# A hybrid convolution and linear-attention block: residual, final norm and store in the convolution's fp32 buffer, gate chain begun one tile earlier

## The reference

```python
h = rms_norm(x, norm_g)
proj = h @ w_in    # c_val, c_gate, c_z, q, k, v, g_lr (16 wide), g_r, m_conv, m_gla
u = c_val * sigmoid(c_gate)
u = depthwise_causal_conv31(u) + conv_b
y_conv = (silu(layer_norm(u)) * silu(c_z)) @ w_conv_out
log_a = log_sigmoid(g_lr @ gate_w2 + gate_b) / 16      # forget gate, per key channel
o = gla_chunked(q, k, v, log_a)   # decayed linear attention, 4 heads; needs exp(+-cumsum(log_a))
y_gla = (rms_norm(o) * silu(g_r)) @ w_gla_out
y = sigmoid(m_conv) * y_conv + sigmoid(m_gla) * y_gla
out = rms_norm(x + y @ w_out, final_g)
```

## Time and profile before

| | us |
|---|---|
| median of 3 runs (lowest, highest) | 1926.79 (1925.39, 1927.14) |
| the profiled execution | 1925.04 |
| its span, core 5, the slowest | 1923.5 |
| the fastest core's span, core 4 | 1907.1 |
| tile 3 to tile 4, first convolution matmul to first convolution matmul | 208.15 |
| first convolution matmul that goes on after the long wait in tile 0 | 301.79 |
| DMA: median from issue to landing of a weight unit, `usc`, one shift, a store | 4.0, 6.9, 5.5, 6.3 |

### The profile page before, as it was taken

How to read it: one execution, slowest core, us unless ns; L and a number is a source line. 1 busy time by engine, 2 the same in 40 slices (tenths; PEclk the granted TensorE clock), 3 DMA queues, 4 the chain that set the end, 5 groups by cost and what they waited for, 6 DMA issues and landing times.

```text
span 1923.5 us, 29181 instructions; the slowest of 8 cores (1907.1 to 1923.5 us)
## 1 busy us (share of the span) xinstructions
PE 1523.7 (79%) x9440; PEld 723.7 (38%) x9440; DVE 643.8 (33%) x991; ACT 655.3 (34%) x1161; POOL 365.2 (19%) x618
## 2 busy tenths in 40 slices
PE   0354006998899889998899889988999889988996
PEld 0121002543344334543354334433454335433442
DVE  1002002433354333432443335433343244332533
ACT  1102002531454125521553145412552155314531
POOL 1101002221032102220222103210222022210311
PEclk9876557998899999999899989999999989998998
DMA  6999998456845495558745594549455874568452
GB/s 119 143 158 147 113 112 232 147 181 181 228 130 188 132 253 157 159 159 227 196 148 176 175 239 130 191 129 279 131 159 159 233 191 147 179 188 226 126 152 74
DMA packets 173795, 326.76 MB, mean 170 GB/s; under 512 B 19776, under 2 KB 60992, under 8 KB 172864
## 3 DMA queue, kind: packets, MB, share of 16 engines
q1 hardware_dynamic: 172224, 299.33, 54.4%
q0 software_dynamic: 1424, 25.56, 11.8%
HBM read 324.69 MB, written 51.12 MB: 195 GB/s over the span
## 4 chain that ended last, share of the span: by engine, by line
PE 60%; DMA 9%; DVE 9%; SPq 8%; ACT 5%; issue 5%; POOL 2%; another core or an unknown queue 0%; DVEq 0%; POOLq 0%; ACTq 0%
PE ps_pb L324 28%; PE ps_pb L334 12%; PE ps_pb L527 8%; PE ps_pb L415 6%; DMA usc<-sb_u 3%; SPq L294 3%; SPq L406 3%; DMA out<-sb_FP 2%; DVE sb_FP L500 2%; DMA w_b<-w 2%; DMA sb_xa<-x 2%; DVE sb_big L468 2%; ACT sb_FP L684 1%; PE ps_pb L660 1%; DVE sb_big L617 1%
## 5 line engine op out<-in xcount | busy, mean ns | idle before, releaser
L324 PE MATMUL ps_pb<-sb_hT,sb_wn 128*128 128x512 bf16 x3136 | 724.2, 387 | 98.8 <-DVE sb_FP L679 48.7
L324 PEld LDWEIGHTS ps_pb<-sb_hT,sb_wn 128*128 128x128 bf16 x3136 | 308.8, 99 | 476.5 <-issue 139.2
L415 PE MATMUL ps_pb<-sb_big,sb_wn 128*32 128x512 bf16 x2048 | 144.3, 431 | 186.5 <-DMA sb_wn<-w_b 120.8
L334 PE MATMUL ps_pb<-sb_big,sb_wn 128*128 128x512 bf16 x1024 | 237.3, 379 | 9.9 <-DVE sb_big L617 9.9
L527 PE MATMUL ps_pb<-sb_wn,sb_hT 128*128 128x512 bf16 x1024 | 227.9, 382 | 9.2 <-DVE sb_u L394 9.2
L454 POOL TENSOR_TENSOR sb_U<-sb_U,sb_FP 128x512 f32<-128x512 f32 x64 | 90.2, 1438 | 471.8 <-DVE sb_FP L440 471.8
L415 PEld LDWEIGHTS ps_pb<-sb_big,sb_wn 128*32 128x32 bf16 x2048 | 62.9, 106 | 259.4 <-issue 221.4
L527 PEld LDWEIGHTS ps_pb<-sb_wn,sb_hT 128*128 128x128 bf16 x1024 | 100.7, 98 | 132.3 <-issue 13.2
L334 PEld LDWEIGHTS ps_pb<-sb_big,sb_wn 128*128 128x128 bf16 x1024 | 98.1, 98 | 124.1 <-issue 13.6
L794 POOL TENSOR_TENSOR sb_yb<-sb_FP 128x512 bf16<-128x512 f32 x64 | 81.0, 1265 | 208.6 <-DVE sb_FP L791 208.5
L394 DVE SCALAR_TENSOR_TENSOR sb_u<-sb_FP,ps_pb 128x512 bf16<-128x512 f32 x64 | 44.0, 687 | 228.2 <-PE ps_pb L324 134.0
(11 more groups left out here) (86 smaller groups left out, 1420.9 us busy)
## 6 DMA issues: line engine op xcount, KB each, us to landing
sb_wn<-w_b SPq DMA_DIRECT2D x776, 256.0 KB, 4.0
sb_big<-usc SPq DMA_DIRECT2D x256, 135.0 KB, 5.5
w_b<-w POOLq DMA_DIRECT2D x17, 1024.0 KB, 54.1
sb_xa<-x SPq DMA_DIRECT2D x32, 512.0 KB, 4.1
sb_FP<-x SPq DMA_DIRECT2D x32, 512.0 KB, 4.7
out<-sb_FP SPq DMA_DIRECT2D x32, 512.0 KB, 6.3
usc<-sb_u SPq DMA_DIRECT2D x64, 136.0 KB, 6.9
w_b<-w POOLq DMA_DIRECT2D x13, 512.0 KB, 27.3
```

The costliest lines, as they stand in the source:

```text
L324: S.op("pe", lambda e, bi=bi, kc=kc, wap=wap: e.matmul(pb[bi][:], lhsT=wap[:, kc * 128:(kc + 1) * 128], rhs=hT[:, hbuf, kc, :], start=(kc ...
L334: S.op("pe", lambda e, bi=bi, kc=kc, wap=wap: e.matmul(pb[bi][:], lhsT=wap[:, kc * 128:(kc + 1) * 128], rhs=src[:, kc, :], start=(kc == 0) ...
L415: S.op("pe", lambda e, cbk=cbk, j=j, b=b, c=c, wap=wap: e.matmul(pb[cbk][32 * b:32 * b + 32, :], lhsT=wap[:, b * 256 + j * 32:b * 256 + j ...
```

## The change

- Residual, square, scale and store of `wout` work in `U1`, in place: `xr_load` brings x into `U1`, four separate blocks, issued in the attention stage after blocks 2 and 3 (two each). Square writes its unused result to `HP`. All four stores are issued in the next tile's GLU stage: block 0 after GLU block 0, block 1 after 1, blocks 2 and 3 after 2.
- `wout` runs over the output's halves first: all four token blocks for half 0, one addition each, then all four for half 1, each followed by `fin` (Square, POOL, scale).
- The low-rank gate projection no longer is a unit: its weights come with the constants (`wglr`, 32 columns a row block), and 8 matmuls in four column groups between two PE drains do it; `gw2` is repeated for the four groups. There are 96 units.
- `gate_in` of the next tile stands at the start of `wout`, `gate_z` with Exp and now Ln after two blocks of half 0. The scans stand after GLU blocks 0 to 3, the subtraction is split into four after blocks 4 to 7, and `decay_exp` follows. Tile 0's stand ahead of the loop. The two wide Exp are issued ahead of the small one.
- The first half of V is evicted by VectorE alone.

```diff
         def gate_in(t):
-            bi = proj_fm(t, U_GLR, t % 2)
+            hbuf = t % 2
+            bi = next_pbank()
+            S.op("pe", lambda e: e.drain())
+            for kc in range(8):
+                q = kc % 4
+                S.op("pe", lambda e, bi=bi, kc=kc, q=q: e.matmul(
+                    pb[bi][32 * q:32 * q + 32, :], lhsT=wglr[:, kc * 32:kc * 32 + 32], rhs=hT[:, hbuf, kc, :],
+                    start=(kc < 4), stop=(kc >= 4), tile_position=(0, 32 * q)),
+                    reads=[B["wglr"], B["hT"][hbuf]], writes=[PB[bi]])
+            S.op("pe", lambda e: e.drain())
             S.op("act", lambda e, bi=bi: e.activation(out=glr[:], in_=pb[bi][:], func=AF.Copy),
                  reads=[PB[bi]], writes=[B["glr"]])
...
+                S.op("act", lambda e, bi=bi, h=h: e.activation(out=FP[:, 4 + h, :], in_=pb[bi][:], func=AF.Exp,
+                                                               scale=-1.0, bias=pp[:, 32 + h:33 + h]),
+                     reads=[PB[bi], B["pp"]], writes=[B["FP"][4 + h]])
+            f4 = FP[:, 4:8, :].rearrange("p a t -> p (a t)")
+            S.op("act", lambda e: e.activation(out=f4, in_=f4, func=AF.Ln, bias=1.0),
+                 reads=B["FP"][4:8], writes=B["FP"][4:8])
+
+        x4 = FP[:, 0:4, :].rearrange("p a t -> p (a t)")
+        f4 = FP[:, 4:8, :].rearrange("p a t -> p (a t)")
+        f3 = f4.rearrange("p (a t) -> p a t", a=16)
+        x3 = x4.rearrange("p (a t) -> p a t", a=16)
+        X4, F4 = B["FP"][0:4], B["FP"][4:8]
+
+        def decay_scan(h):
+            S.op("dve", lambda e: e.tensor_tensor_scan(
+                out=FP[:, 4 + h, :], data0=scanm[:], data1=FP[:, 4 + h, :], initial=0.0, op0=ALU.mult, op1=ALU.add),
+                reads=[F4[h], B["scanm"]], writes=[F4[h]])
+
+        def decay_sub(h):
+            a = slice(4 * h, 4 * h + 4)
+            S.op("dve", lambda e: e.tensor_tensor(out=x3[:, a, :], in0=f3[:, a, :],
+                                                  in1=f3[:, a, 63:64].to_broadcast([128, 4, 128]),
+                                                  op=ALU.subtract), reads=[F4[h]], writes=[X4[h]])
+
+        def decay_exp():
...
+            S.op("act", lambda e: e.activation(out=f4, in_=x4, func=AF.Exp, scale=1.0 / 16.0), reads=X4, writes=F4)
+            S.op("act", lambda e: e.activation(out=x4, in_=x4, func=AF.Exp, scale=-1.0 / 16.0), reads=X4, writes=X4)
             S.op("act", lambda e: e.activation(out=gar[:], in_=gar[:], func=AF.Exp, scale=-1.0 / 16.0),
                  reads=[B["gar"]], writes=[B["gar"]])
-            S.op("act", lambda e: e.activation(out=f4, in_=x4, func=AF.Exp, scale=-1.0 / 16.0), reads=X4, writes=F4)
-            S.op("act", lambda e: e.activation(out=x4, in_=x4, func=AF.Exp, scale=1.0 / 16.0), reads=X4, writes=X4)
...
-                if split and s % 2 == 0:
+                if split and (half == 0 or s % 2 == 0):
...
+        def u1v(s):
+            return U1[:, 2 * s:2 * s + 2, :].rearrange("p a t -> p (a t)")
+            S.op("sp", lambda e: e.dma_start(out=u1v(s), in_=x_d[r0:r0 + 128, :]),
+                 writes=B["U1"][2 * s:2 * s + 2], dma_sem=xr_sems[s])
+            S.op("sp", lambda e: e.dma_start(out=out_d[r0:r0 + 128, :], in_=u1v(s)),
+                 reads=B["U1"][2 * s:2 * s + 2], writes=[B["outdone"][s]], dma_sem=out_sems[s])
+
+        def fin(t, s):
+            col = 8 + (t * 4 + s) % 8
+            ub = B["U1"][2 * s:2 * s + 2]
+            hv = HP[:, 0:2, :].rearrange("p a t -> p (a t)")
+            S.op("act", lambda e: e.activation(out=hv, in_=u1v(s), func=AF.Square, accum_out=ssx[:, col:col + 1]),
+                 reads=ub, writes=[B["HP"][0], B["HP"][1], B["ssx"][col]])
+            S.op("pool", lambda e: e.tensor_scalar(
+                out=ssx[:, col:col + 1], in0=ssx[:, col:col + 1], scalar1=1.0 / D, scalar2=EPS,
+                op0=ALU.mult, op1=ALU.add), reads=[B["ssx"][col]], writes=[B["ssx"][col]])
+            S.op("pool", lambda e: e.tensor_tensor(
+                out=ssx[:, col:col + 1], in0=ssx[:, col:col + 1], in1=pp[:, 26:27], op=ALU.pow),
+                reads=[B["ssx"][col], B["pp"]], writes=[B["ssx"][col]])
+            S.op("dve", lambda e: e.scalar_tensor_tensor(
+                out=u1v(s), in0=u1v(s), scalar=ssx[:, col:col + 1], in1=Gf[:], op0=ALU.mult, op1=ALU.mult),
+                reads=ub + [B["ssx"][col], B["Gf"]], writes=ub)
...
+        def wout(t, more):
+            def mm(bi, sl, s, kc):
+                wap, wbuf = sl[kc // 2]
                 S.op("pe", lambda e: e.matmul(
                     pb[bi][:], lhsT=yb[:, kc, s * 128:(s + 1) * 128],
                     rhs=wap[:, (kc % 2) * 512:(kc % 2) * 512 + 512], start=(kc == 0), stop=(kc == 7)),
                     reads=[wbuf, B["yb"][kc]], writes=[PB[bi]])
 
+            def add(bi, half, s):
+                ub = B["U1"][2 * s + half]
+                S.op("dve", lambda e: e.scalar_tensor_tensor(
+                    out=U1[:, 2 * s + half, :], in0=pb[bi][:], scalar=0.5, in1=U1[:, 2 * s + half, :],
+                    op0=ALU.mult, op1=ALU.add), reads=[PB[bi], ub], writes=[ub])
+
+            if more:
+                gate_in(t + 1)
+            sl = units(t, U_WO(0), 4)
+            b01 = [next_pbank(), next_pbank()]
+            for s in range(2):
+                for kc in range(7):
+                    mm(b01[s], sl, s, kc)
+            for s in range(2):
+                mm(b01[s], sl, s, 7)
+                add(b01[s], 0, s)
+            if more:
+                gate_z(t + 1)
+            for s in (2, 3):
+                bi = next_pbank()
+                for kc in range(8):
+                    mm(bi, sl, s, kc)
+                add(bi, 0, s)
+            sl = units(t, U_WO(1), 4)
             for s in range(4):
+                bi = next_pbank()
+                for kc in range(8):
+                    mm(bi, sl, s, kc)
+                add(bi, 1, s)
+                fin(t, s)
...
                 glu(t, c)
-                if t > 0 and c == 0:
-                    store(t - 1, 3)
+                if c < 4:
+                    decay_scan(c)
+                else:
+                    decay_sub(c - 4)
+                if t > 0 and c in (0, 1, 2):
+                    store(t - 1, c)
+                    if c == 2:
+                        store(t - 1, 3)
                 if c >= 1:
                     shift(c - 1)
             if t == 0:
                 issue_casts(N_U)
-            gate_in(t)
+            decay_exp()
             shift(7)
             wide_tm(t, U_V(0), vT, B["vT"], AF.Copy, True)
-            gate_z(t)
-            gate_decay(t)
             wide_tm(t, U_V(1), vT, B["vT"], AF.Copy, True)
...
-            xr_load(t, 0)
-            xr_load(t, 1)
+                if s >= 2:
+                    xr_load(t, 2 * s - 4)
+                    xr_load(t, 2 * s - 3)
```

More of the change, by code:

```diff
@@ L224, in mk @@
                 B[name] = [Buf("%s%d" % (name, i)) for i in range(n)]
-        for nm in ["cst", "identb", "maskb", "onesb", "scanm", "Gn", "Gf", "pp", "gw2", "glr",
+        for nm in ["cst", "identb", "maskb", "onesb", "scanm", "Gn", "Gf", "pp", "gw2", "glr", "wglr",
                    "tail", "gar", "junk"]:
@@ L234, in build_nc @@
         mk("w_b", N_U)
-        mk("outdone", 2)
+        mk("outdone", 4)
         B["Rbf"] = [[Buf("Rbf%d_%d" % (i, h)) for h in range(4)] for i in range(2)]
@@ L274, in build_nc @@
         S.op("dve", lambda e: e.tensor_copy(out=maskb[:], in_=cst[:, 128:256]), reads=[B["cst"]], writes=[B["maskb"]])
+        S.op("dve", lambda e: e.tensor_copy(out=wglr[:], in_=cst[:, 256:512]), reads=[B["cst"]], writes=[B["wglr"]])
         S.op("dve", lambda e: e.tensor_scalar(out=pp[:, 32:36], in0=pp[:, 32:36], scalar1=-1.0, scalar2=0.0,
@@ L375, in pre_pe @@
                 reads=[PB[6]], writes=[B["hT"][hbuf]])
-        xr_sems = [newsem("xr0"), newsem("xr1")]
-        out_sems = [newsem("o0"), newsem("o1")]
+        xr_sems = [newsem("xr%d" % i) for i in range(4)]
+        out_sems = [newsem("o%d" % i) for i in range(4)]
         u4_sems = [[newsem("u4s_%d_%d" % (i, g)) for g in range(4)] for i in range(8)]
@@ L487, in gate_z @@
                      reads=[B["glr"], B["gw2"]], writes=[PB[bi]])
-                S.op("act", lambda e, bi=bi, h=h: e.activation(out=FP[:, h, :], in_=pb[bi][:], func=AF.Exp, scale=-1.0,
-                                                               bias=pp[:, 32 + h:33 + h]),
-                     reads=[PB[bi], B["pp"]], writes=[B["FP"][h]])
-        def gate_decay(t):
-            f4 = FP[:, 0:4, :].rearrange("p a t -> p (a t)")
-            x4 = FP[:, 4:8, :].rearrange("p a t -> p (a t)")
-            f3 = f4.rearrange("p (a t) -> p a t", a=16)
-            x3 = x4.rearrange("p (a t) -> p a t", a=16)
-            F4, X4 = B["FP"][0:4], B["FP"][4:8]
-            S.op("act", lambda e: e.activation(out=f4, in_=f4, func=AF.Ln, bias=1.0), reads=F4, writes=F4)
-            for h in range(4):
```

(31 more changed lines are left out.)

72 lines of the change are left out of this document (15 added, 57 removed).

## The result

| | before | after |
|---|---|---|
| median (lowest to highest) | 1926.65 (1925.39 to 1927.14), 4 runs | 1858.39 (1854.75 to 1880.22), 4 runs |
| span of the slowest core, profiled execution | 1923.5, core 5 | 1856.7, core 2 |
| spans of the eight cores | 1907.1 to 1923.5 | 1835.5 to 1856.7 |
| granted clock of the slowest core | 0.915 | 0.936 |

The ratio is 0.967, 95% interval 0.9596 to 0.9745. The changed kernel is 68 us faster, where the prediction had 85: 1858 lies in its range of 1820 to 1880, 17 us above its 1841. Times of the experiments are medians of the runs within 1.5% of the kernel's fastest; in the others four or all eight cores were granted a lower clock and took some per cent longer.

A forecast was written before the change was run, and what follows sets the result against it. PE, busy 79%, was taken as the bound, stopped in two gaps at each of seven crossings. 80.5 us there, 2.8 in tile 0 and 1.8 at the end sum to 85 saved: 1841 forecast, range 1820 to 1880.

The forecast's parts named there:

- The second gap: PE's 7.93 us stop before the convolution; moving the gate chain out of the V stage was to gain 12.5 us a crossing.
- the slow clock at the convolution's start: Half-speed clock after the stop before the convolution; its end was to gain 2.4 us a crossing.
- The 0.5 taken for transfers: Convolution waiting for its shifted copies; 0.5 us lost per crossing, between 0 and 5.
- The first gap: PE's 6.93 us stop in the GLU stage; a store's wait was to become 4.7 and 2.6 us for VectorE's order.
- the in-place chain: Residual, square and scale in place in wout; the store's wait goes, VectorE's order replaces it, 0.5 us worse a crossing.
- 11.5 us a crossing: Net gain from tile to tile: 12.5 - 0.5 - 0.5, times 7 crossings, 80.5 us.
- tile 0: First tile's long wait for casts; one unit fewer gives 2.4 us and shift(7) passing one load 0.4, together 2.8.
- Table loads: Two more ScalarE table loads a tile, four in all, hidden at zero cost; without cover 1.3 us a tile.
- Rival 2: The u4 transfers take over the convolution's wait, 3.5 us plus 2.4 of clock a crossing; 1883, chance 0.18.
- Rival 3: Both PE gaps go, another 7.3 + 1.0 us a crossing; 1783, chance 0.08.
- Rivals 4: Stores in the GLU stage choke the shifts, so the kernel gets slower; 1981, chance 0.05.
- 5: Nothing gained, the convolution would wait for the shifts behind VectorE anyway; 1925, chance 0.03.

The follow-up runs named there:

- e3: Changed kernel with the gate chain back in the V stage and the first half of V evicted by both engines; 1877.28, ratio 0.9785.
- e6: Kernel before the change with only the PSUM bank ring of a tile started four banks later; 1880.79, ratio 0.9776.
- e7: e3 with the bank ring started two banks later, so the first GLU units take the late banks; two runs, 1896.93 and 1893.15.
- e5: The changed kernel again, unedited; 1851.83, ratio 0.9635.
- e8: Changed kernel with 8 unused weight units more cast behind tile 0's last cast; 1867.4, ratio 0.9711.
- e2: Changed kernel with the PSUM bank ring of a tile started two banks later, VectorE's order kept; 1814.88, ratio 0.9457.
- e1: Changed kernel with each block's scale issued after the next block's addition in the second half of the output projection; 1789.4, ratio 0.9328.
- e4: Changed kernel with each store issued right after its scale in the output projection, none in the GLU stage; 1851.9, ratio 0.9673.
- e9: e1 with each store issued right after its scale in the output projection, none in the GLU stage; 1786.26, ratio 0.93.

## Why the prediction held, and where it was off

**The second gap, right.** L415 no longer waits for the value evictions. V to C fell by 8.10; the prediction's terms for it are 0.87 + 7.93 - 0.4 = 8.4. The difference is the pause at PE's drain before the convolution, 0.74 instead of 0.41; what makes this drain the longer one, no run here tells. Of the 2.4 for the slow clock at the convolution's start, C to Q shows 1.68. The 0.5 taken for transfers did not come (0.01). Short waits between C and Q grew by 0.3 us on the mean, and the remaining 0.4 I can't name. That the gain goes with the gate work and its place is shown by e3, where the wait is back at 7.9; e6 shows that another start of the ring only moves it. e3 undoes two things at once, though, the place of the gate work and VectorE's eviction of the first half of V, and no run parts these.

**The first gap, right in mechanism and size.** Predicted: additions 4.3 apart, measured 4.30, 4.57 and 4.29. Waits of 4.7 and 2.6, measured 4.63 and 1.13, because the first unit at half speed fills part of the second. Predicted: the second block's first unit (CG(1)) 26.7 us after W, measured 1064.24 + 1.73 - 1039.54 = 26.4. The clock loss behind the second wait was taken as 1.0; it is 0 in the crossing shown and 1.3 on average (31.53 - 30.2). The clock of 1.00 before the fall that the prediction names stands in none of the earlier trace rows; the trace before has it, 1.00 from 1083 to 1084 and 0.50 from 1085 to 1086 on core 5. Square of block 0 at 1051.03 was not held by Ln, which ended at 1050.11.

```profile
1048.20 1.91 ACT L502 ACTIVATE sb_FP<-sb_FP 128x2048 f32<-128x2048 f32 x1
1051.03 1.06 ACT L671 ACTIVATE sb_HP<-sb_U 128x1024 bf16<-128x1024 f32 x1 [0.92 <-DVE sb_U L693]
```

**Wrong: to whom the gain was credited.** The prediction's step is the in-place chain, "0.5 us worse", with all 12.5 given to the gate work. The 0.5 was worked out with the gate's matmuls and its five allocations in it. e3 shows the parts: the in-place half alone gains 5.3 us a crossing, and moving the gate work adds 4.4 to that. Moving it saves 9.6 us from V to Q (44.09 in e3, 34.54 after) and costs 4.6 from W to V (47.20, 51.80) and 0.5 ahead of W. Of the 4.6, 0.5 are PE's own gate work (1.8 us from W to V here, 1.3 in e3) and 2.1 the longer wait for the additions ((39.3 - 24.3) / 7), because the GLU units get the late banks first. The rest, 2.0, I put down to the slow clock in and behind a longer idle stretch. e7 reproduces those waits from the ring alone. With the banks dealt as the prediction had them, e7's W to V is 50.67 against 52.14 before: the in-place half with the small gate unit (0.4) is 1.5 us better there and 2.4 over the crossing, not 0.5 worse. The sum hardly suffered, since both parts were changed at once. Anyone who took only half of this change by the prediction's account would have been misled.

**Wrong in size: 11.5 us a crossing.** By the means it is 9.7 (207.29 to 197.63), 1.8 less. Of this 0.9 is the choice of the core: on core 5 the stretch from W to V took 53.1 us at this crossing (with a gap of 6.9; it is 6.8 to 7.2 in five of that core's seven, where the others have about 6), on the mean 52.1. The prediction's figure for this stretch, 53.1 - 1.73 + 0.5 = 51.9, was met: 51.8. Another 0.4 is the drain ahead of the gate projection, which stands before W, so that the terms from W on missed it (the branches' stretch grew from 43.42 to 43.83). The rest is 0.3 at the drain before the convolution and 0.2 between C and Q. On the slowest cores it is 72.2 / 7 = 10.3, hence 72 us instead of 80.5 (208.1 on core 5 before and 197.8 on core 2 after, means of their seven).

**Wrong in size: tile 0.** Predicted 2.8 gained. On the mean over the cores `wout` of tile 0 begins at 431.2 instead of 433.3. That is no proof of a gain: the changed kernel again (e5) has 427.6 there, and e6, with all 97 units, 426.3. And the kernel's time is that of the slowest core, and on core 2 tile 0 ended 7.0 us later than on core 5 before. These starts spread over 21 us among the cores of one run (421.5 to 442.7), 12 before. e8's price of a unit, 1.9 us, is below the 2.45 taken. Together with the crossings, this adds up to the 18 us: 8.3 there, 9.8 here, 0.2 at the tail (1.6 for 1.8). The 7.0 lost here did not come again: in e5 the slowest core begins at 435.1, and the ratio is 0.9635. So part of the 17 us by which 1841 was missed is the scatter of tile 0. Why the spread in tile 0 is what it is, no run here tells.

**Table loads, right.** Four a tile, and free:

```profile
L390 ACT ACT_TABLE_LOAD x8 | 10.3, 1283 | 0.3 <-PE ps_pb L325 0.2
L449 ACT ACT_TABLE_LOAD x8 | 10.3, 1283 | 24.1 <-DVE sb_FP L446 24.1
L461 ACT ACT_TABLE_LOAD x8 | 10.3, 1283 | 14.6 <-DVE sb_U L458 14.6
L498 ACT ACT_TABLE_LOAD x7 | 9.0, 1283 | 24.8 <-PE ps_pb L495 24.8
```

At L498 the load starts at 1044.39 and its activation at 1045.69, 1.30 later, so no further drain shows, as in the earlier trace rows. The half microsecond that the rule of the Trainium skill (ScalarE: Activation LUTs, the section What ACT_TABLE_LOAD costs) would have added to Square did not come.

**The rivals.** Rival 2 (the u4 transfers take over) did not happen in the changed kernel: 6.3 us in all. It is what e2 meets once the first gap is gone and VectorE is still late. Rival 3 (both gaps go, 1783) is wrong for this change, but its price of 8.3 us a crossing was about right: in e1, where both do go, the crossing is 7.9 shorter. Rivals 4 (the stores choke the shifts) and 5 are refuted by the result, and e4 and e9 show besides that the stores cost nothing there.
